# The last two output units of the second cross attention, its layer norm and the first gate unit, cut into halves of 256 tokens

## What is computed

```python
def first_block(x, mem, ...):
    ...
    for l in range(DEPTH):
        ...
        y = memory_cross_attention(x, mem_n, xa_wq[l], xa_wk[l], xa_wv[l], xa_wo[l])   # ends with o @ w_o
        x = layer_norm(ALPHA * x + y, ln_xa_g[l], ln_xa_b[l])
        y = swiglu_ffn(x, ffn_wg[l], ffn_wu[l], ffn_wd[l])    # (silu(x @ w_gate) * (x @ w_up)) @ w_down
        ...

def layer_norm(x, g, b):
    mu = jnp.mean(xf, axis=-1, keepdims=True)
    var = jnp.mean(jnp.square(xf - mu), axis=-1, keepdims=True)
    y = (xf - mu) * lax.rsqrt(var + LN_EPS) * g + b
```

## Time and profile before

| what | value |
| --- | --- |
| median of 3 runs | 2499.72 us (2494.28 to 2500.06) |
| the profiled execution, its own time | 2501.4 us |
| its span on the core | 2499.6 us |
| busy share of the span: TensorE, VectorE, ScalarE | 98%, 59%, 35% |
| share of TensorE in the chain that ended last | 89% |

### The profile page before, as it was taken

One profiled execution on the slowest core, in us unless ns is written; L12 is line 12 of the kernel. 1 busy time (PEld: TensorE's weight loads), 2 busy tenths in 40 slices (PEclk: granted clock), 3 DMA queues, 4 the chain that ended last, 5 costly groups with the idle time before them and its releaser, 6 DMA issues.

```text
span 2499.6 us, 28907 instructions
## 1 busy us (share of the span) xinstructions
PE 2443.4 (98%) x11306; PEld 1992.4 (80%) x11306; DVE 1469.3 (59%) x2029; ACT 865.9 (35%) x1146; POOL 22.1 (1%) x36
## 2 busy tenths in 40 slices
PE   8999999999999999999999999999999999999998
PEld 7888877788887876788887688888888877888886
DVE  6898735644445835544445634656665776655666
ACT  4344533422223733422222533422222465322222
POOL 0000000000000000000000000000000000000000
PEclk9999999999999999999999899999999999999999
DMA  5222322323222221222232121233333211232221
GB/s 191 88 85 85 101 68 70 111 99 101 101 88 80 102 68 68 85 101 86 98 101 100 60 99 51 68 94 118 120 105 120 101 52 63 89 101 101 98 87 67
DMA packets 38891, 229.19 MB, mean 92 GB/s; under 512 B 8821, under 2 KB 8837, under 8 KB 12448
## 3 DMA queue, kind: packets, MB, share of 16 engines
q1 hardware_dynamic: 31824, 220.22, 25.9%
q0 software_dynamic: 6992, 7.92, 1.3%
HBM read 222.82 MB, written 5.24 MB: 91 GB/s over the span
## 4 chain that ended last, share of the span: by engine, by line
PE 89%; DVE 7%; ACT 3%; issue 1%; DMA 0%; DVEq 0%; SPq 0%; ACTq 0%
PE bank L677 88%; DVE w_lo L1887 1%; ACT w_hi L1358 1%; DVE xs L2000 1%; ACT xs L1435 1%; DVE xl L1902 1%; DVE xs L2020 1%; DVE cacc L2125 0%; DVE hs L2176 0%; ACT xh L1377 0%; PE bank L1296 0%; DVE sum_x L1909 0%; PE bank L991 0%; DVE spare_lo L1884 0%; DVE sum_q L1916 0%
## 5 line engine op out<-in xcount | busy, mean ns | idle before, releaser
L1887 DVE TENSOR_TENSOR w_lo<-w_raw,w_hi 128x2048 fp32r<-128x2048 f32 x201 | 460.4, 2291 | 382.7 <-ACT w_hi L1358 382.4
L677 PE MATMUL bank<-xh,w_hi 128*128 128x512 f32 x1416 | 560.4, 396 | 16.8 <-DVE xl L1902 7.0
L677 PE MATMUL bank<-xl,w_hi 128*128 128x512 f32 x1416 | 554.6, 392 | 0.0
L677 PE MATMUL bank<-xh,w_lo 128*128 128x512 f32 x1416 | 554.4, 392 | 0.0
L1358 ACT ACTIVATE w_hi<-w_raw 128x2048 fp32r<-128x2048 f32 x201 | 383.5, 1908 | 386.3 <-PE bank L677 384.7
L1972 DVE TENSOR_TENSOR xs<-xs,bank 128x512 f32<-128x512 f32 x448 | 294.3, 683 | 104.0 <-PE bank L677 103.1
L677 PEld LDWEIGHTS bank<-xh,w_hi 128*128 128x128 f32 x1416 | 268.1, 189 | 80.0 <-issue 11.5
L677 PEld LDWEIGHTS bank<-xl,w_hi 128*128 128x128 f32 x1416 | 268.2, 189 | 56.6 <-issue 1.6
L677 PEld LDWEIGHTS bank<-xh,w_lo 128*128 128x128 f32 x1416 | 267.9, 189 | 56.4
L677 PE MATMUL bank<-yh,w_hi 128*128 128x512 f32 x576 | 226.8, 394 | 0.0
L677 PE MATMUL bank<-yh,w_lo 128*128 128x512 f32 x576 | 224.3, 389 | 0.0
(11 more groups left out here) (276 smaller groups left out, 2943.6 us busy)
## 6 DMA issues: line engine op xcount, KB each, us to landing
w_raw<-weights_in SPq DMA_DIRECT2D x205, 1024.0 KB, 4.8
rel_scratch<-vt POOLq DMA_DIRECT2D x8, 384.0 KB, 19.2
bias<-rel_scratch POOLq DMA_DIRECT2D x8, 256.0 KB, 3.1
y_out<-xs SPq DMA_DIRECT2D x8, 256.0 KB, 2.0
xs<-x_in SPq DMA_DIRECT2D x3, 512.0 KB, 8.0
mk<-mem_in POOLq DMA_DIRECT2D x1, 1024.0 KB, 9.7
window<-consts_in POOLq DMA_DIRECT2D x1, 576.0 KB, 6.1
xs<-x_in SPq DMA_DIRECT2D x2, 256.0 KB, 3.9
```

Source lines behind the costliest of these rows:

```text
L677: return pe.matmul(dst, a, b, start=start, stop=stop)
L1887: dve.tensor_tensor(w_lo[:, c % 2, :], w_raw[:, c % 2, :], w_hi[:, c % 2, :].bitcast(F32), ALU.subtract)\
```

## The change

For l = 1 only, units 2 and 3 of the output projection run as four half units of 256 tokens, in the order unit 2 tokens 0 to 255, unit 3 tokens 0 to 255, unit 3 tokens 256 to 511, unit 2 tokens 256 to 511 (`OUT_HALVES`; n = 0 to 3). Each half unit writes both of its feature tiles into one bank. The norm runs once per half of the tokens, on pairs of feature tiles of 256 tokens (so an elementwise instruction still has 512 elements per partition), and the gate unit runs the first half of the tokens, then the second. TensorE issues the norm sums of the first half inside half unit 2, and those of the second half inside the first half of the gate unit, ahead of its tiles k = 1 and k = 2. The gate unit's weights go to the third slot, which lets their split stand directly behind that of unit 3. The high part of unit c + 5 waits for the end of half unit 2 (`ahead=1`).

```diff
-SPARE = [UNITS["xq0"], UNITS["ffn0"], UNITS["xq1"]]
+SPARE = [UNITS["xq0"], UNITS["ffn0"], UNITS["xq1"], UNITS["ffn1"]]
+OUT_HALVES = [(2, 0), (3, 0), (3, 1), (2, 1)]
+HALF = [slice(0, T // 2), slice(T // 2, T)]
...
+            def half_means(half):
+                key, a = ("xan1", "mean", half), HALF[half]
+                wait_free(pe, key)
+                seen.next("half_summed")
+                mm(bank(key)[:, 0:T // 2], ones[:, :], sum_x[:, a], True, False)
+                for n in (2 * half, 2 * half + 1):
+                    j = OUT_HALVES[n][0]
+                    wait_drained(pe, ("xo1", j, "half", half))
+                k = 2 * j
+                mm(bank(key)[:, 0:T // 2], ones[:, :], xs[:, k, a], False, False)
+                full(mm(bank(key)[:, 0:T // 2], ones[:, :], xs[:, k + 1, a], False, True), key)
...
+            def out_halves():
...
+                for n, (j, half) in enumerate(OUT_HALVES):
+                    c, a, key = UNITS["xo1"] + j, HALF[half], ("xo1", j, "half", half)
+                    pe.wait_ge(w_lo_ready, c + 1)
+                    wait_free(pe, key)
+                    for m in range(2):
+                        for k in range(KT):
+                            if n == 2 and k == 4:
+                                (half_means, half_squares)[m](0)
+                            last = mm3(bank(key)[:, HALF[m]], weights(c, k * 256 + m * P, P), (xh[:, k, a], xl[:, k, a]),
+                                       k == 0, k == KT - 1)
+                    full(last, key)
+
+            def gate_halves(c, keys_):
...
+                for half in range(2):
+                    a = HALF[half]
+                    for k in range(KT):
+                        if k % 2 == 0:
+                            tile_ready(k)
+                        if half == 0 and k in (1, 2):
+                            (half_means, half_squares)[k - 1](1)
+                        for m, key in enumerate(keys_):
+                            last = mm3(bank(key)[:, a], weights(c, k * 256 + m * P, P), (xh[:, k, a], xl[:, k, a]),
+                                       k == 0, k == KT - 1)
...
+            def halves_norm():
...
+                def half_pair(half, p):
+                    a = HALF[half]
+                    seen.next("zn_ready")
+                    for k in (2 * p, 2 * p + 1):
+                        last = act.activation(xs[:, k, a], xs[:, k, a], ACT.Identity, scale=col("xa_g1", k), bias=col("xa_b1", k))
+                    give(last, "xn_ready")
+                    own_xn()
+                    give(act.activation(xh[:, 2 * p:2 * p + 2, a], xs[:, 2 * p:2 * p + 2, a], ACT.Copy), "x_hi")
+
+                split_hi(c + 3)
+                split_hi(c + 4)
+                seen.next("sq_used")
+                half_square(0)
+                half_square(1)
+                half_mean(0)
+                half_root(0)
+                half_pair(0, 0)
+                half_pair(0, 1)
+                seen.next("half_summed")
+                half_square(2)
+                split_hi(c + 5, ahead=1)
+                half_pair(0, 2)
+                half_pair(0, 3)
+                wait_full(act, ("xan1", "sq", 0))
+                half_square(3)
+                half_mean(1)
+                half_root(1)
+                for p in range(4):
+                    half_pair(1, p)
...
+            def halves_norm():
...
+                split_lo(c + 3)
+                wait_drained(dve, ("xo1", 1, 1))
+                add_to_sums(3, True, xs_at)
+                split_lo(c + 4)
+                half_add(0)
+                half_sums(0)
+                half_add(1)
+                seen.next("mean_ready")
+                for p in range(2):
+                    half_centre(0, p)
+                half_variance(0)
+                half_centre(0, 2)
+                half_centre(0, 3)
+                seen.next("rstd_ready")
+                half_scale(0, 0)
+                half_scale(0, 1)
+                half_rest(0, 0)
+                half_scale(0, 2)
+                half_rest(0, 1)
+                half_add(2)
+                half_scale(0, 3)
+                half_sums(2)
+                half_rest(0, 2)
+                split_lo(c + 5)
+                half_rest(0, 3)
+                half_add(3)
+                seen.next("mean_ready")
+                for p in range(2):
+                    half_centre(1, p)
+                half_variance(1)
+                half_centre(1, 2)
+                half_centre(1, 3)
+                seen.next("rstd_ready")
+                half_scale(1, 0)
+                for p in range(1, 4):
+                    half_scale(1, p)
+                    half_rest(1, p - 1)
+                half_rest(1, 3)
```

More of the change, by code:

```diff
@@ L289, in plan_banks @@
         fill((f"xo{l}", 0, 1), 5, UNITS[f"xo{l}"])
-        for j in range(1, 4):
-            pair(f"xo{l}", j)
-        norm(f"xan{l}")
+        if l == 0:
+            for j in range(1, 4):
+                pair("xo0", j)
+            norm("xan0")
+        else:
+            pair("xo1", 1)
+            c = UNITS["xo1"]
+            for b, (j, half) in enumerate(OUT_HALVES):
+                fill(("xo1", j, "half", half), b, c + 2 + b % 2 if half else None)
+            for half in range(2):
+                fill(("xan1", "mean", half), 6 - 2 * half)
+                fill(("xan1", "sq", half), 7 - 2 * half)
         if l == 0:
@@ new lines, in half_squares @@
+            def half_squares(half):
+                key = ("xan1", "sq", half)
+                wait_free(pe, key)
+                seen.next("half_sq", 2)
+                mm(bank(key)[:, 0:T // 2], ones[:, :], sum_q[:, HALF[half]], True, False)
+                mm(bank(key)[:, 0:T // 2], ones[:, :], sq[:, 0, HALF[1]], False, False)
+                full(mm(bank(key)[:, 0:T // 2], ones[:, :], sq[:, 1, HALF[1]], False, True), key)
+            def out_halves():
+                seen.skip("sq_used", 3)
+                seen.skip("sq_ready", 4)
+                for n, (j, half) in enumerate(OUT_HALVES):
+                    c, a, key = UNITS["xo1"] + j, HALF[half], ("xo1", j, "half", half)
+                    pe.wait_ge(w_lo_ready, c + 1)
+                    wait_free(pe, key)
+                    for m in range(2):
[5 more added lines that the diff above has]
+                    full(last, key)
@@ new lines, in gate_halves @@
+            def gate_halves(c, keys_):
+                pe.wait_ge(w_lo_ready, c + 1)
+                for key in keys_:
+                    wait_free(pe, key)
+                for half in range(2):
+                    a = HALF[half]
[7 more added lines that the diff above has]
+                                       k == 0, k == KT - 1)
+                            if half and k == KT - 1:
+                                full(last, key)
@@ L1005, in up @@
                     for which in ("g", "u") if gate else ("u",):
+                        if name == "ffn1" and ready:
+                            gate_halves(c, [(name, tag, which, m) for m in range(2)])
+                            ready = None
+                            c += 1
+                            continue
                         pe.wait_ge(w_lo_ready, at(i, per, c + 1))
@@ L1145, in _ @@
                 out_tiles(l, range(4, KT))
[L1146 to L1149, removed]
+                feature_unit(f"xo{l}", 1)
                 if l == 0:
+                    feature_unit("xo0", 2)
+                    last_unit("xo0", 3)
+                    residual_norm("xan0", pair_keys("xo0"))
                     filler(FILLER["xan0"])
+                else:
+                    out_halves()
                 chunks(f"ffn{l}", tile_ready)
@@ L2031, in normalise, with pair_of, both_tiles, half_add @@
                     split_lo(unit + 3 if stage else unit + 1)
+            def halves_norm():
+                c = UNITS["xo1"]
+                H = T // 2
+                centred = {}
+                def pair_of(t, p, half):
+                    return t[:, 2 * p:2 * p + 2, HALF[half]]
+                def both_tiles(ap):
+                    return ap.unsqueeze(1).broadcast_to([P, 2, H])
+                def half_add(n):
+                    j, half = OUT_HALVES[n]
+                    key = ("xo1", j, "half", half)
+                    x2 = pair_of(xs, j, half)
+                    wait_full(dve, key)
+                    free(dve.scalar_tensor_tensor(x2, x2, ALPHA, bank(key)[:, :].rearrange("p (m t) -> p m t", m=2),
+                                                  ALU.mult, ALU.add), key)
+                    wait_drained(dve, key)
+                def half_sums(n):
+                    j, half = OUT_HALVES[n]
+                    a = HALF[half]
+                    own("sq_used")
+                    for m in range(2):
+                        steps.wait()
+                        steps.step(dve.tensor_tensor(sum_x[:, a], sum_x[:, a], xs[:, 2 * j + m, a], ALU.add))
```

(32 more changed lines are left out.)

33 lines of the change are left out of this document (27 added, 6 removed).

## The result

| | median | runs | lowest to highest |
| --- | --- | --- | --- |
| before | 2499.72 us | 12 | 2494.28 to 2501.73 |
| changed | 2504.57 us | 12 | 2499.62 to 2508.15 |

The ratio is 1.0022, with a 95% interval from 1.0015 to 1.0030: by it the change makes the kernel slower by 5.5 us, 3.7 to 7.5 (the two medians lie 4.9 us apart; the ratio is that of the means). The prediction was 6.5 us slower, 2506.2 us, with a range from 2495 to 2511.

What follows compares the result with a forecast made beforehand. TensorE, busy 98% of the span, bounds the kernel. Added: 1.9 + 1.7 work, 1.2 + 7.4 + 1.1 + 0.8 waits and restarts, 1.8 clock, less 9.4: 6.5 us slower, 2506.2 us, range 2495 to 2511.

Steps and rivals of the forecast that it cites:

- the gaining rival: VectorE reaches half_add(3) in time, right behind its half unit: 3 us faster, or 4.6 if pairs keep up; 18%.
- TensorE's own work: Output projection, gate unit and norm sums: 144 cuts cost 1.9 us, twelve sums instead of four 1.7 us more.
- Point 1: Output projection: after unit 2's first half TensorE waits 1.2 us for unit 3's low weights, ready at 977.15.
- Points 3 and 4: First half's chain brings pair 0 in time; VectorE's strict program order delays half_add(3) to 1005.2, its half unit full since 997.5.
- Point 5: Gate unit: after tile 0 TensorE stands at the second half's mean sums until 1006.1, 7.4 us idle.
- Point 6: Second half's norm chain: TensorE waits 1.1 us, then takes pairs at ScalarE's 1.65 us; up unit starts at 1020.9.
- the bound of 3 us: Upper bound if VectorE's or ScalarE's two-piece patterns (2 tiles x 256) cost as two instructions, about 20 on the path.
- Point 7: Granted clock of 0.50 after the long idle time charges 1.8 us on the second half's sums; bounds nothing to 2.9.
- The sum: Up unit starts at 1022.7 against 1016.15, so the kernel is 6.5 us slower.
- D: Distance from the start of unit 2 to the start of the up unit: 45.8 us before, some 52 predicted.
- The 0.8: Part of the predicted loss, listed with 1.2, 7.4 and 1.1 us as new waits and restarts.
- the 9.4 us "lost" before: Kernel before, around the second cross attention's norm: 6.2 us idle plus 3.2 of slow gate unit, all the change can reach.

Runs made afterwards that it cites:

- the experiment: The changed kernel with half_add(3) moved directly behind half_sums(2) in VectorE's program; 2499.4 us, ratio 1.0003 to the kernel before.
- TensorE kept busy: The changed kernel plus 52 matmuls of 256 columns, results unused, filling TensorE's waits; 2503.78 us, ratio 1.0019 to the kernel before.
- the new order: The changed kernel's halves with the programs of TensorE, VectorE and ScalarE reordered, arithmetic unchanged; 2496.14 us, ratio 0.9990 to the kernel before; second time 2494.99 us, 0.9986.
- third slot alone: The kernel before with only the gate unit's weights put in the third slot; one execution, no ratio given, 45.82 us from unit 2 to up unit.

## Why the prediction was right, step by step

The sign, the size and the mechanism held. The wide range, 2495 to 2511 us, would prove little, as it took in most of the gaining rival; the forecast's own range of 4.5 to 8.5 us slower held too. By its own points:

- *TensorE's own work.* The cut was put at 0.013 us and measured 0.013. The twelve sums were taken at 0.45 us each; where they ran together at full clock they stood 0.43 apart. That is 0.2 us too much.
- *Point 1, the wait for unit 3's weights.* 1.2 us foretold, with its restart; TensorE idled 0.95 and started at 977.09, where 977.24 was foretold (all times of the changed trace lie 0.11 earlier). The restart of 0.2 us, for which the prediction names no row, was 0.16 here: 0.06 from the weights to the first matmul, and 0.10 more than usual to the next start.
- *Points 3 and 4, the order of VectorE.* `half_add(2)` foretold for 996.8, seen at 996.67; `half_add(3)` foretold for 1005.1, seen at 1004.96. This is the step on which the result hangs, and moving that one line took 4.4 us off.
- *Point 5, the idle time.* 7.4 us foretold, 1.91 + 5.31 = 7.2 seen.
- *Point 6, the second chain.* A wait of 1.1 us for its first pair, 0.85 seen; pairs at 1.65 us, 1.64 to 1.67 seen. The two-piece patterns cost nothing: VectorE's take 0.69 us and start 0.60 apart, like contiguous ones, which settles the bound of 3 us at its lower end.
- *Point 7, the clock.* 1.8 us foretold, 1.7 and 1.95 seen.
- *The sum.* D 52.4 foretold, 51.95 and 52.24 seen; 6.5 us slower foretold, 5.5 measured. The 0.8 in it that stands beside the waits is not worked out there; three pairs at 1.65 instead of 1.44 and one restart of 0.2 give it.

What the prediction had wrong, though it didn't decide: the rival in which VectorE adds in time. It said that "all of point 6 would move up" with the addition, 7.7 us for 7.7. In the experiment the addition stood 5.4 us earlier (998.07 - 968.73 = 29.3 us behind the start of unit 2, against 34.7), and D fell by 4.4, of which 1.7 is the clock's: the chain moved by 2.7. The rival took the addition for the only late thing; behind it stood the square of the same half unit on ScalarE, in the same kind of order. That is 1.8 of the missing 2.7 us: the second half's square sums began 33.6 us behind the start of unit 2, where they began at 37.2 with TensorE kept busy. The other 0.9 is VectorE, which came to the variance 2.4 us behind the start of those sums and not 1.5, as unit c + 5's low weights, a low part and two centres stood ahead of it. Only with all three orders rewritten did D fall by 9.5. And the 9.4 us "lost" before were not 6.2 of idle time and 3.2 of slow clock: filling the gap changed nothing, so the slow clock was hidden behind the chain of the norm.

## What to carry to other kernels

Cutting a stage in two, so that one half's work covers the other's chain, buys only what the orders of all the engines let through: mark in each engine's program how long a finished thing lies before its consumer comes to it (here a half unit lay finished for 7.8 us, and taking a weight split that nobody was waiting for out of its way cut TensorE's wait by 3.0). A large instruction that isn't urgent, here 1.9 us on one engine and 2.3 on the next, belongs in a hole and not ahead of the chain. And where two executions differ in stages that the change doesn't touch, measure the changed stretch between two landmarks of its own: here the totals lay 0.7 us apart where the stretch had lost 6.1.

## What the runs showed of the hardware that I had not expected

The granted clock is touchy about short waits. With the addition moved forward TensorE waited 1.9, 1.6 and 1.7 us within 13.4 us of the trace and kept its full clock; in the new order with the sums at the old place it waited 2.2 and 2.0 us, with 6.6 us of work between, and 0.50 followed for 3.4 us. With unit c + 5's weights out of the way it waited 1.9 and 2.35 us with one sum between, and 0.50 followed as well. Why the one and not the others I have not tried to tell apart. And the same stretch of the linear attention ran at 0.50 or at 1.00 in executions whose programs are alike there. That makes the largest part of the scatter behind the change: from the start of the up unit to the end of the span it took 1478.1 to 1478.3 us in the three profiles in which the linear attention had no stretch at 0.50 (changed, third slot alone, new order the second time), and 1480.7 to 1483.8 us in the ten others, the kernel before among them.
